# One key tile, scores against plain rotary products, and V by pairs in a latent-attention stage

## The chip, the cores and the metric

The kernel runs on one core of a Trainium2 chip. Its engines are TensorE (PE, the matmuls), VectorE (DVE), ScalarE (ACT), GpSimd (POOL) and SyncE (SP, which issues the DMAs). The metric is the device time of one execution in microseconds; three executions of the kernel before took 1416.03, 1418.67 and 1420.28 us. What differs by less than 0.3% (4.3 us) from the median is no measurable change.

## The reference, cut to what matters

```python
# SEQ 512, D_MODEL 1024, 8 heads, 128 plain + 64 rotary query/key dims, V 128, float32
def apply_rope(x, cos, sin):                       # x: ..., 64
    x1, x2 = x[..., :32], x[..., 32:]
    return concatenate([x1 * cos - x2 * sin, x2 * cos + x1 * sin], -1)

def mla(h, cos, sin, w_down, q_norm, w_uq, kv_norm, w_ukv, w_o):
    d = h @ w_down                                  # 1024 -> 384 + 128 + 64
    cq = rms_norm(d[..., :384], q_norm)
    ckv = rms_norm(d[..., 384:512], kv_norm)
    k_rope = apply_rope(d[..., 512:], cos, sin)     # one rotary key for all heads
    q = (cq @ w_uq).reshape(B, S, 8, 192)           # 128 plain, 64 rotary (apply_rope)
    kv = (ckv @ w_ukv).reshape(B, S, 8, 256)        # 128 key, 128 value
    ...                                             # causal softmax(q k / sqrt(192)) v
    return o.reshape(B, S, 1024) @ w_o

x = x + mla(rms_norm(x, norm_mix[1]), ...)          # between two SwiGLU stages
```

Around this stage stand, in program order, a pooling mixer, a SwiGLU feed-forward (1024 to 2816 and back), the attention stage, a second feed-forward, and a second block with two more attentions, gates and an output norm.

## The kernel before, in words

Activations are kept transposed: 128 features on the partitions, the 512 tokens along the row. Every float32 product is made of three matmuls (`triple`, L1590 to L1594): each operand is split into a rounded part `hi` (a copy by ACT into float32r) and the rest `lo` (a subtraction by DVE), and hi·hi, hi·lo and lo·hi are summed in PSUM. So a tile of 128 outputs over 8 input tiles (`chunk`) is 24 matmuls of 512 columns. Weights come in units of 128x2048 numbers: SP loads a unit when the one before the last is split, ACT makes `w_hi` (`split_hi`), DVE `w_lo` (`split_lo`); two buffers of each.

The attention stage, `mla` on each engine, has four parts.

1. Down-projection. Three weight units give six output tiles in banks 0 to 5: the key/value latent, one query latent tile, two tiles of the rotary key (the same 64 columns twice, plain and with its halves swapped, so that `key·cos + swapped·sin` is one rotated key on partitions 0 to 63 and again on 64 to 127), two more query latent tiles. DVE takes `1/rms` of the residual by a reciprocal (L1116) and multiplies each tile by it on its way out of PSUM (`down_q`, L1119, L1124).
2. First projections of a pair of heads, `FIRST_PROJ` (L308): plain key and query of head 0 (`kn0`, `qn0`), rotary queries of both heads (`u`) and the same with halves swapped (`us`), key of head 1 (`kn1`). A query or rotary tile takes 9 matmuls of 512 columns, a key tile 3, a value tile 12 of 128 columns (four token blocks of three). They alternate between banks 0 and 1; a projection waits until the one before the last is read.
3. 32 attention steps, four per head. Step s = (head h, ii) takes query block i = 3 - ii: `scores` (three matmuls of the plain part, three of the rotary part over 64 partitions, L1768, and a causal mask), with (i+1)·128 columns each, into one of three banks; the softmax is made by DVE (`row_max`), ACT (`softmax_exp`) and DVE (`normalise`); `turn(s-3)` transposes the probabilities of the step three before; ACT and DVE split them (`turned_hi`, `turned_lo`); `values` multiplies a whole head, in the first step of the head after next. At the end of a step come the projections for later heads that `after_step(h, ii)` lists (L310). Each engine goes through its own list in order; semaphores join them. A scores step waits for the exponentials of three steps before, and a turn for the `lo` of two turns before.
4. Output projection: 8 chunks of 24 matmuls, the first two begun between the last turns.

Names used below: `kn`, `qn`, `v` and a digit are the plain key, plain query and value of the even (0) or odd (1) head of a pair. `root`, `squares`, `sq_sum` are working tiles; `sq_sum` holds the partial sums of squares of the residual. `row_max` waits on `att_scored`, `turn` on `att_probs` and `att_lo`.

## Time and profile before

| | us |
|---|---|
| median of three runs | 1418.67 |
| the profiled execution's own time | 1417.11 |
| its span on the core | 1415.3 |
| PE busy in the span | 1352.3 (96%) |
| PE weight loads busy (beside the matmuls) | 1110.8 |
| DVE busy | 789.2 |
| ACT busy | 537.0 |
| POOL busy | 32.1 |

In the profile a PE row gives the time at which a matmul was issued and its modelled duration, which overlaps the next one's: what a matmul costs in a stream is the distance between two starts. L1592, L1593 and L1594 are the three lines of the helper `triple`, so its matmuls are told apart by the tiles behind the arrow. `[0.59 <-DVE pt_lo L1212]` behind a row is idle time of that engine just before it, and who ended it. `64*128` and `128*128` name the part of the array that a matmul uses. PEclk is the granted clock as a share of 2.4 GHz, so 0.50 is 1.2 GHz.

The attention stage runs from 404.22 us (first matmul of the down-projection) to about 600 us. Outside it the change touches only a few small constants that POOL writes at the start: POOL's last one is written at 0.90 us in the kernel before, and ACT's first read of one is at 10.34 us.

### The profile page before, as it was taken

Reading aid. Unit: us, or ns where it says so; the run is one execution under the profiler, and the core shown is the slowest. Engines: PE = TensorE matmul, PEld = TensorE weight load, DVE = VectorE, ACT = ScalarE, POOL = GpSimd, SP = SyncE. Lnnn points to the kernel's source line nnn. Section 1 sums busy time; section 2 is a strip of 40 time slices with the busy share of each in tenths; the row PEclk is TensorE's granted clock in tenths of the full one; section 3 lists DMA queues with packets and bytes.
Section 4 is the critical chain, followed back from the end, with each engine's and each line's share of the span. In section 5 each row is a group of like instructions: output and inputs, shape, how many; then the busy total and the mean of one; then the engine's idle time right before and its main releaser. Section 6 shows DMA issues by size and latency. Waiting matters only on the chain.

```text
span 1415.3 us, 16583 instructions
## 1 busy us (share of the span) xinstructions
PE 1352.3 (96%) x6315; PEld 1110.8 (78%) x6315; DVE 789.2 (56%) x1093; ACT 537.0 (38%) x754; POOL 32.1 (2%) x28
## 2 busy tenths in 40 slices
PE   6999999999999999899999999999999999977997
PEld 5788888888887777788888888888887787855876
DVE  5644445444456677465444454454775577876554
ACT  6522233233343444343222222334224345556334
POOL 6000000000000000000000000000000000020000
PEclk9999999999998999999999999999999999988999
DMA  6122322222342111032233222333542111102321
GB/s 207 60 94 96 107 89 89 93 82 89 98 119 55 31 44 47 32 117 90 96 98 103 89 82 82 104 99 104 152 144 82 60 31 45 61 0 89 117 78 60
DMA packets 130409, 120.75 MB, mean 85 GB/s; under 512 B 23020, under 2 KB 127416, under 8 KB 130104
## 3 DMA queue, kind: packets, MB, share of 16 engines
q1 hardware_dynamic: 130360, 120.08, 26.8%
q8 instruction: 33, 0.54, 0.2%
q14 instruction: 16, 0.13, 0.0%
HBM read 115.88 MB, written 4.19 MB: 85 GB/s over the span
## 4 chain that ended last, share of the span: by engine, by line
PE 86%; DVE 8%; ACT 3%; issue 2%; SPq 0%; DMA 0%; DVEq 0%; ACTq 0%
PE psum L1592 26%; PE psum L1593 26%; PE psum L1594 26%; DVE w_lo L1003 1%; PE psum L1936 1%; PE psum L1922 1%; PE psum L1908 1%; PE psum L1778 1%; ACT w_hi L577 1%; PE psum L1636 1%; PE psum L1769 0%; PE psum L2012 0%; PE psum L1628 0%; PE psum L1994 0%; DVE du L1269 0%
## 5 line engine op out<-in xcount | busy, mean ns | idle before, releaser
L1592 PE MATMUL psum<-xg_hi,w_hi 128*128 128x512 f32 x1080 | 429.2, 397 | 2.9 <-DVE xg_lo L1506 2.9
L1594 PE MATMUL psum<-xg_hi,w_lo 128*128 128x512 f32 x1080 | 420.7, 390 | 0.0
L1593 PE MATMUL psum<-xg_lo,w_hi 128*128 128x512 f32 x1080 | 420.6, 389 | 0.0
L1592 PEld LDWEIGHTS psum<-xg_hi,w_hi 128*128 128x128 f32 x1080 | 203.1, 188 | 46.0 <-DVE xg_lo L1506 3.4
L1594 PEld LDWEIGHTS psum<-xg_hi,w_lo 128*128 128x128 f32 x1080 | 202.8, 188 | 42.6
L1593 PEld LDWEIGHTS psum<-xg_lo,w_hi 128*128 128x128 f32 x1080 | 203.1, 188 | 40.8 <-issue 1.4
L1066 DVE TENSOR_TENSOR w_lo<-w_raw,w_hi 128x2048 fp32r<-128x2048 f32 x42 | 96.3, 2292 | 154.4 <-ACT w_hi L629 154.4
L1090 DVE TENSOR_TENSOR w_lo<-w_raw,w_hi 128x2048 fp32r<-128x2048 f32 x32 | 73.3, 2292 | 115.9 <-ACT w_hi L648 115.9
L1592 PE MATMUL psum<-act_hi,w_hi 128*128 128x512 f32 x352 | 137.2, 390 | 0.0
L1593 PE MATMUL psum<-act_lo,w_hi 128*128 128x512 f32 x352 | 137.0, 389 | 0.0
L1594 PE MATMUL psum<-act_hi,w_lo 128*128 128x512 f32 x352 | 136.9, 389 | 0.0
L629 ACT ACTIVATE w_hi<-w_raw 128x2048 fp32r<-128x2048 f32 x42 | 80.4, 1914 | 142.0 <-PE psum L1594 142.0
L1003 DVE TENSOR_TENSOR w_lo<-w_raw,w_hi 128x2048 fp32r<-128x2048 f32 (+2 forms) x60 | 95.1, 1586 | 29.5 <-ACT w_hi L577 29.5
L648 ACT ACTIVATE w_hi<-w_raw 128x2048 fp32r<-128x2048 f32 x32 | 61.2, 1913 | 117.6 <-PE psum L1594 117.6
L577 ACT ACTIVATE w_hi<-w_raw 128x2048 fp32r<-128x2048 f32 x40 | 76.4, 1909 | 25.8 <-PE psum L1594 25.7
L1592 PEld LDWEIGHTS psum<-act_hi,w_hi 128*128 128x128 f32 x352 | 66.1, 188 | 14.3 <-DVE w_lo L1090 0.6
L1594 PEld LDWEIGHTS psum<-act_hi,w_lo 128*128 128x128 f32 x352 | 66.1, 188 | 13.8
L1593 PEld LDWEIGHTS psum<-act_lo,w_hi 128*128 128x128 f32 x352 | 66.1, 188 | 13.5
L632 ACT ACTIVATE root<-squares 128x512 f32<-128x512 f32 x44 | 27.8, 632 | 100.4 <-DVE squares L1071 100.4
L634 ACT ACTIVATE act_hi<-squares 128x512 f32 (+1 forms) x44 | 27.8, 631 | 89.0 <-DVE squares L1076 89.0
L1073 DVE TENSOR_TENSOR squares<-psum,rstd 128x512 f32<-128x512 f32 x44 | 30.4, 691 | 50.4 <-PE psum L1594 50.4
L1079 DVE TENSOR_TENSOR act_lo<-squares,act_hi 128x512 f32 (+1 forms) x44 | 30.5, 693 | 39.9 <-ACT act_hi L634 39.9
(358 smaller groups left out, 1778.4 us busy)
## 6 DMA issues: line engine op xcount, KB each, us to landing
w_raw<-in_ffn_w_gate SPq DMA_DIRECT2D x22, 1024.0 KB, 5.0
w_raw<-in_ffn_w_up SPq DMA_DIRECT2D x22, 1024.0 KB, 4.9
w_raw<-in_w_in SPq DMA_DIRECT2D x16, 1024.0 KB, 5.5
w_raw<-in_ffn_w_down SPq DMA_DIRECT2D x16, 768.0 KB, 4.8
w_raw<-in_ffn_w_down SPq DMA_DIRECT2D x16, 640.0 KB, 4.3
w_raw<-in_mla_w_o SPq DMA_DIRECT2D x4, 1024.0 KB, 5.0
w_raw<-in_w_out SPq DMA_DIRECT2D x4, 1024.0 KB, 5.2
...
```

What stands on the lines that cost most here:

```text
L577: act.activation(w_hi[:, n % 2, :], raw(n), ACT.Copy).then_inc(hi_sem, 1)
L629: act.activation(w_hi[:, n % 2, :], raw(n), ACT.Copy).then_inc(hi_sem, 1)
L632: act.activation(gate_s, gate_z, ACT.Silu).then_inc(ga, 1)
L648: act.activation(w_hi[:, n % 2, :], raw(n), ACT.Copy).then_inc(hi_sem, 1)
L1003: lo = dve.tensor_tensor(w_lo[:, n % 2, c], raw(n)[:, c], w_hi[:, n % 2, c].bitcast(F32), ALU.subtract)
L1066: dve.tensor_tensor(w_lo[:, n % 2, :], raw(n), w_hi[:, n % 2, :].bitcast(F32), ALU.subtract).then_inc(lo_sem, 1)
L1073: dve.tensor_tensor(up_z, bank[2 + c][:, :], rstd[:, :], ALU.mult).then_inc(gd, 1)
L1079: dve.tensor_tensor(act_lo[:, f, :].rearrange("p a t -> p (a t)"), gate_z, act_hi[:, f, :].bitcast(F32).rearrange("p a t -> p (a t)"), ALU ...
L1090: dve.tensor_tensor(w_lo[:, n % 2, :], raw(n), w_hi[:, n % 2, :].bitcast(F32), ALU.subtract).then_inc(lo_sem, 1)
L1592: pe.matmul(o, wh, xh, start=start, stop=False, skip_group_check=True)
L1593: pe.matmul(o, wh, xl, start=False, stop=False, skip_group_check=True)
L1594: return pe.matmul(o, wl, xh, start=False, stop=stop, skip_group_check=True)
```

## The change

- **One key tile.** The down-projection makes five tiles, not six: one tile holds the 64 rotary key columns and, on the other 64 partitions, the same with swapped halves. From it come `K·cos` and `K·sin` as one 128-partition key that pairs with an unrotated product on the query side. Unit `KEY_UNIT` has 1024 columns to split instead of 2048.
- **Rotary scores from plain query times cos and sin.** The projection `us` is gone. From `u` (two heads of 64) DVE makes, for each head, `q·cos` on partitions 0 to 63 and `q·sin` on 64 to 127: four 64x512 products in place of two 128x512 products and a sum. ACT and DVE then split one 128-partition tile per head (`rotary(h)`), where one tile served two heads. The rotary scores run over all 128 partitions. A unit of head weights has 13·128 columns instead of 16·128.
- **Norms absorb the reciprocal root.** Query and key/value latents are no longer multiplied by `1/rms` of the residual; it would cancel in their own norms but for the epsilon, which comes in as a second accumulating matmul (`eps_share` times `sq_sum`) in both statistics. ACT and DVE read the latents in PSUM directly.
- **V by pairs.** A value projection makes two token blocks of both heads of a pair (`va`, `vb`): six matmuls of 256 columns, two such per pair, where there were two of twelve with 128 columns.
- **First steps reordered.** `FIRST_PROJ` is now `kn0, kn1, va, vb, u, qn0, qn1` in five banks, so that pair 0 has no projection left for heads 0 and 1; `after_step` and the two DVE/ACT places of `rotary` are new. On ACT a square of the key/value tile now stands ahead of the load of the square-root table.

On PE, in head 0, before: the end of `v0`'s twelve matmuls of 128 columns (`w_hi,ckv_hi`), then `scores(3)` (plain part from `xg_hi`, rotary part from `kr_hi`, mask), then `turn(0)`:

```order
L1592 MATMUL psum<-w_hi,ckv_hi 128x128
L1593 MATMUL psum<-w_lo,ckv_hi 128x128
L1594 MATMUL psum<-w_hi,ckv_lo 128x128
L1592 MATMUL psum<-xg_hi 128x128
L1593 MATMUL psum<-xg_lo,xg_hi 128x128
L1594 MATMUL psum<-xg_hi,xg_lo 128x128
L1592 MATMUL psum<-kr_hi,xg_hi 128x128
L1593 MATMUL psum<-kr_lo,xg_hi 128x128
L1594 MATMUL psum<-kr_hi,xg_lo 128x128
L1769 MATMUL psum<-causal,ident_r 128x128
L1778 MATMUL psum<-ident,probs 128x128 x4
```

On PE, the same place now: the end of `scores(2)`, then `scores(3)`, then `turn(0)`:

```order
L1650 MATMUL psum<-kr_lo,xg_hi 128x256
L1651 MATMUL psum<-kr_hi,xg_lo 128x256
L1831 MATMUL psum<-causal,ident_r 128x128
L1649 MATMUL psum<-xg_hi 128x128
L1650 MATMUL psum<-xg_lo,xg_hi 128x128
L1651 MATMUL psum<-xg_hi,xg_lo 128x128
L1649 MATMUL psum<-kr_hi,xg_hi 128x128
L1650 MATMUL psum<-kr_lo,xg_hi 128x128
L1651 MATMUL psum<-kr_hi,xg_lo 128x128
L1831 MATMUL psum<-causal,ident_r 128x128
L1840 MATMUL psum<-ident,probs 128x128 x4
```

`qn1` and `v0` no longer stand between the scores of steps 2 and 3 of head 0; they are made before `scores(0)`.

On DVE, in the second step of head 1, before: the rotary tile of the next pair (`u` times cos, `us` times sin, sum, `lo`), then `row_max`, `normalise` and `turned_lo` of the next step, then the `lo` of `qn0` and `v1`:

```order
L1167 TENSOR_TENSOR squares<-psum,cos_t 128x512
L1171 TENSOR_TENSOR squares<-psum,sin_t 128x512
L1173 TENSOR_TENSOR squares<-squares 128x512
L1180 TENSOR_TENSOR xg_lo<-squares,xg_hi 128x512
L1195 TENSOR_REDUCE row_top<-psum 128x1
L1197 TENSOR_TENSOR neg_max<-row_top,rq 128x1
L1202 RECIPROCAL row_inv<-row_sum 128x1
L1204 TENSOR_SCALAR probs<-probs,row_inv 128x384
L1212 TENSOR_TENSOR pt_lo<-psum,pt_hi 128x2x128
L1180 TENSOR_TENSOR xg_lo<-psum,xg_hi 128x512 x2
```

On DVE, the same place now:

```order
L1219 TENSOR_TENSOR squares<-psum,cos_t 64x512
L1220 TENSOR_TENSOR squares<-psum,sin_t 64x512
L1219 TENSOR_TENSOR squares<-psum,cos_t 64x512
L1220 TENSOR_TENSOR squares<-psum,sin_t 64x512
L1250 TENSOR_REDUCE row_top<-psum 128x1
L1252 TENSOR_TENSOR neg_max<-row_top,rq 128x1
L1257 RECIPROCAL row_inv<-row_sum 128x1
L1259 TENSOR_SCALAR probs<-probs,row_inv 128x384
L1267 TENSOR_TENSOR pt_lo<-psum,pt_hi 128x2x128
L1230 TENSOR_TENSOR xg_lo<-squares,xg_hi 128x512
L1225 TENSOR_TENSOR xg_lo<-psum,xg_hi 128x512
```

Two 128x512 products, a sum and a `lo` became four 64x512 products, and the `lo` of the rotary tile has moved behind `turned_lo` of the next step; `v1` is gone from here.

The diff, cut to what the text speaks of:

```diff
-        pieces = ((0, 2 * P, 2 * P), (256, 64, r0), (320, 64, r0), (384, 32, r0 + 32), (416, 32, r0), (448, 32, r0 + 32), (480, 32, r0),
-                  (512, 2 * P, 0))
+        pieces = ((0, 2 * P, 2 * P), (256, 64, r0), (320, 32, r0 + 32), (352, 32, r0), (512, 2 * P, 0))
...
 
         QUERY_TILES = (2, 0, 1)
-
-        FIRST_PROJ = ("kn0", "qn0", "u", "us", "kn1")
+        KEY_UNIT = FIRST["mla_down"] + 1
+
+        FIRST_PROJ = ("kn0", "kn1", "va", "vb", "u", "qn0", "qn1")
+        FIRST_BANKS = (5, 7, 0, 1, 2, 3, 0)
 
         def after_step(h, ii):
 
+            pr, last = h // 2, h + 1 == HEADS
             if h % 2 == 0:
-                return tuple((h // 2, what) for what in (("kn1",), (), ("qn1", "v0"), ())[ii] if h or what not in FIRST_PROJ)
-            return tuple((h // 2 + int(what != "v1"), what) for what in (("kn0",), ("u", "us"), ("qn0", "v1"), ())[ii] if what == "v1" or h + 1 < HEADS)
+                return () if h == 0 else (((pr, "kn1"),), (), ((pr, "qn1"),), ())[ii]
+            this = ((pr, "va"),), ((pr, "vb"),), (), ()
+            following = ((pr + 1, "kn0"),), ((pr + 1, "u"),), ((pr + 1, "qn0"),), ()
+            return (() if last else following[ii]) + (this[ii] if pr else ())
+
+        def rotary_head(h, ii):
+
+            if h % 2 == 0:
+                return h + 1 if h and ii == 1 else None
+            return h + 1 if ii == 2 and h + 1 < HEADS else None
 
         PROJ_ORDER = [(0, what) for what in FIRST_PROJ] + [x for h in range(HEADS) for ii in range(NB) for x in after_step(h, ii)]
 
+        def proj_bank(idx):
...
-                act.activation(w_hi[:, n % 2, :], raw(n), ACT.Copy).then_inc(hi_sem, 1)
+                if n == KEY_UNIT:
+                    hi = act.activation(tiles256(w_hi[:, n % 2, :], 8)[:, :, 0:P], tiles256(raw(n), 8)[:, :, 0:P], ACT.Copy)
+                else:
+                    c = slice(0, head_thirds(n)[-1])
+                    hi = act.activation(w_hi[:, n % 2, c], raw(n)[:, c], ACT.Copy)
+                hi.then_inc(hi_sem, 1)
...
+                act.wait_ge(sem("mla_down_done"), 1)
+                act.activation(squares[:, 0, :], bank[0][:, :], ACT.Square, scale=ROOT_KVL).then_inc(sem("kv_square"), 1)
...
+                    act.activation(cq_hi[:, t, :], bank[idx][:, :], ACT.Copy, scale=gain("mla_q_norm", t)).then_inc(sem("cq_act"), 1)
+                    act.activation(squares[:, n - 1, :] if n else sq_sum2[:, :], bank[idx][:, :], ACT.Square, scale=ROOT_QL).then_inc(sem("cq_act"), 1)
...
+                for what in FIRST_PROJ[:-1]:
+                    proj(0, what)
+                rotary(0)
...
+                dve.scalar_tensor_tensor(cos_s, cos_t[:, :], eps_col[:, 3:4], rstd[:, :], ALU.mult, ALU.mult).then_inc(step, 1)
+                dve.tensor_tensor(sin_s, sin_t[:, :], rstd[:, :], ALU.mult).then_inc(step, 1)
...
+                dve.tensor_tensor(down_q[:, 2, :], bank[2][:, :], cos_s, ALU.mult).then_inc(step, 1)
+                dve.tensor_tensor(root[0:64, :], bank[2][64:128, :], sin_s[64:128, :], ALU.mult).then_inc(step, 1)
+                dve.tensor_tensor(root[64:128, :], bank[2][0:64, :], sin_s[0:64, :], ALU.mult).then_inc(step, 1)
+                dve.wait_ge(step, 5)
+                dve.tensor_tensor(down_q[:, 2, :], down_q[:, 2, :], root[:, :], ALU.add).then_inc(*mark("kr_ready"))
...
+                        for e in range(2):
+                            r = slice(64 * e, 64 * e + 64)
+                            dve.tensor_tensor(squares[0:64, e, :], ps[r, :], cos_t[r, :], ALU.mult).then_inc(sem("rope_turned"), 1)
+                            sine = dve.tensor_tensor(squares[64:128, e, :], ps[r, :], sin_t[r, :], ALU.mult)
+                            sine.then_inc(*((done, 1) if e else (sem("rope_turned"), 1)))
                         return
...
+                def rotary(h):
+
+                    dve.wait_ge(sem("rope_hi"), h + 1)
+                    dve.tensor_tensor(xg_lo[:, QR + h % 2, :], squares[:, h % 2, :], xg_hi[:, QR + h % 2, :].bitcast(F32), ALU.subtract)\
+                       .then_inc(sem("rope_lo"), 1)
...
-                    pe.wait_ge(lo_sem, n + 1)
+                for idx, (j, c) in enumerate(((0, 1), (0, 0), (1, 0), (2, 0), (2, 1))):
...
+                    if idx == 1:
+                        pe.wait_ge(sem("kv_square"), 1)
+                        pe.matmul(bank[5][:, :], ones[:, :], squares[:, 0, :], start=True, stop=False)
+                        pe.matmul(bank[5][:, :], eps_share[:, :], sq_sum[:, :], start=False, stop=True).then_inc(*mark("kv_stat"))
...
+                            for j in range(2):
+                                tok = slice((2 * int(what == "vb") + j) * P, (2 * int(what == "vb") + j + 1) * P)
+                                o = ps[:, 2 * j * P:(2 * j + 2) * P].rearrange("p (e d) -> p e d", e=2)
+                                mm = triple(o, ckv_hi[:, tok], ckv_lo[:, tok], wh[:, 10:13:2, :], wl[:, 10:13:2, :], True, True)
...
-                            mm = pe.matmul(bank[6][:, 2 * i:2 * i + 2], sq_sum[:, i * P:(i + 1) * P], ones[:, 0:2], start=True, stop=True)
+                            tok = slice(i * P, (i + 1) * P)
+                            pe.matmul(bank[6][:, 2 * i:2 * i + 2], sq_sum2[:, tok], ones[:, 0:2], start=True, stop=False)
+                            mm = pe.matmul(bank[6][:, 2 * i:2 * i + 2], sq_sum[:, tok], eps_share[:, 0:2], start=False, stop=True)
...
-                    r = slice(64 * hs, 64 * hs + 64)
-                    qh, ql = rotary_q(h // 2)
-                    triple(o, qh[r, q], ql[r, q], kr_hi[r, k], kr_lo[r, k], False, False)
+                    triple(o, xg_hi[:, QR + hs, q], xg_lo[:, QR + hs, q], kr_hi[:, k], kr_lo[:, k], False, False)
```

## Rows read from the trace of the kernel before

**Rows 1.** The page's part 4: the chain that ended last, shares by engine.

```profile
PE 86%; DVE 8%; ACT 3%; issue 2%; SPq 0%; DMA 0%; DVEq 0%; ACTq 0%
```

**Rows 2.** Stretches: from:to, length, busy us (instructions) of PE, weight loads, DVE, ACT, POOL, granted clock, DMA.

```profile
438.66:450.08 11.42, 8.83 (x42) 6.85 (x41) 6.36 (x11) 4.88 (x8) 0.00 (x0) 0.99 0.24 51
450.08:480.89 30.81, 30.70 (x133) 23.64 (x134) 17.32 (x42) 11.53 (x25) 0.00 (x0) 0.78 0.15 35
480.89:511.75 30.86, 30.26 (x169) 24.30 (x168) 21.75 (x55) 14.83 (x34) 0.00 (x0) 1.00 0.11 35
511.75:542.63 30.88, 30.25 (x167) 24.32 (x166) 22.06 (x55) 14.85 (x34) 0.00 (x0) 1.00 0.10 35
```

**Rows 3.** Matmuls in order of time, 421 to 451 us: start, duration, line, tiles, shape.

```profile
421.45 1.02 PE L1717 MATMUL psum<-squares,ones 128*128 128x512 f32 x2
...
422.54 0.39 PE L1593 MATMUL psum<-xg_lo,w_hi 128*128 128x512 f32 x1
...
433.22 0.39 PE L1592 MATMUL psum<-xg_hi,w_hi 128*128 128x512 f32 x1
...
438.66 0.39 PE L1592 MATMUL psum<-ckv_hi,w_hi 128*128 128x512 f32 x1
...
450.08 0.76 PE L1592 MATMUL psum<-xg_hi 128*128 128x512 f32 x1 [2.31 <-DVE xg_lo L1180]
```

**Rows 4.** The same view, one 512-column scores step (head 1): plain, rotary, mask, turn.

```profile
466.12 0.40 PE L1594 MATMUL psum<-xg_hi,xg_lo 128*128 128x512 f32 x1
466.45 0.49 PE L1592 MATMUL psum<-kr_hi,xg_hi 64*128 64x512 f32 x1
466.78 0.39 PE L1593 MATMUL psum<-kr_lo,xg_hi 64*128 64x512 f32 x1
467.01 0.39 PE L1594 MATMUL psum<-kr_hi,xg_lo 64*128 64x512 f32 x1
467.34 0.33 PE L1769 MATMUL psum<-causal,ident_r 128*128 128x128 f32 x1
```

**Rows 5.** The same view: plain scores of 256 columns, and a value projection of 128 columns.

```profile
474.89 0.28 PE L1593 MATMUL psum<-xg_lo,xg_hi 128*128 128x256 f32 x1
475.01 0.28 PE L1594 MATMUL psum<-xg_hi,xg_lo 128*128 128x256 f32 x1
...
478.21 0.27 PE L1593 MATMUL psum<-w_lo,ckv_hi 128*128 128x128 f32 x1
478.32 0.28 PE L1594 MATMUL psum<-w_hi,ckv_lo 128*128 128x128 f32 x1
```

**Rows 6.** The same view: a turn that waits for DVE in the even head of a pair.

```profile
489.44 0.30 PE L1778 MATMUL psum<-ident,probs 128*128 128x128 f32 x1 [0.59 <-DVE pt_lo L1212]
```

**Rows 7.** Groups of 395 to 625 us: count, busy us, mean ns, idle before them.

```profile
L1180 DVE TENSOR_TENSOR xg_lo<-psum,xg_hi 128x512 fp32r<-128x512 f32 x24 | 16.6, 691 | 20.5 <-ACT xg_hi L687 20.2
L1212 DVE TENSOR_TENSOR pt_lo<-psum,pt_hi 128x512 fp32r<-128x512 f32 x8 | 5.5, 685 | 0.0
L1003 DVE TENSOR_TENSOR w_lo<-w_raw,w_hi 128x768 fp32r<-128x768 f32 x4 | 3.8, 946 | 0.0
L687 ACT ACTIVATE xg_hi<-psum 128x512 fp32r<-128x512 f32 x24 | 14.0, 596 | 9.0 <-PE psum L1594 9.0
```

**Rows 8.** Stretches, columns as in rows 2: around the falls of the granted clock.

```profile
448.00:450.00 2.00, 0.00 (x0) 0.00 (x0) 1.24 (x2) 1.11 (x2) 0.00 (x0) 0.96 0.00 0
450.00:452.00 2.00, 1.92 (x4) 1.20 (x5) 0.69 (x1) 0.00 (x0) 0.00 (x0) 0.50 0.00 0
...
462.00:464.00 2.00, 2.00 (x13) 1.90 (x12) 0.69 (x1) 0.60 (x1) 0.00 (x0) 0.63 0.00 0
...
562.00:566.00 4.00, 3.41 (x26) 3.02 (x26) 3.03 (x10) 1.63 (x5) 0.00 (x0) 0.99 0.32 115
...
566.00:568.00 2.00, 2.00 (x10) 1.76 (x10) 1.39 (x4) 1.20 (x4) 0.00 (x0) 0.50 0.00 0
...
586.00:590.00 4.00, 2.37 (x9) 1.61 (x9) 1.88 (x3) 2.51 (x2) 0.00 (x0) 1.00 0.00 0
```

More of the change, by code:

```diff
@@ L690, in mla @@
[L690 to L697 removed]
+                    h = 2 * pr + int(what[-1] == "1")
@@ L714, in mla @@
-                proj(0, "qn0")
+                act.activation(rq[:, 0, :], bank[6][:, 0:2 * NB], ACT.Sqrt, scale=128.0 + ROPE, bias=eps_col[:, 1:2]).then_inc(*mark("rq_root"))
+                proj(0, "qn1")
+                rotary(1)
                 act.preload_act_table(ACT.Exp)
-                for what in FIRST_PROJ[2:]:
-                    proj(0, what)
                 def softmax_exp(s):
@@ L1185, in mla @@
                 dve.wait_ge(*at("rq_ready"))
-                for what in FIRST_PROJ[1:]:
-                    proj(0, what)
+                proj(0, "qn1")
+                rotary(1)
                 def row_max(s):
@@ new lines, in proj @@
+                    if what[0] in "qu":
+                        if what == "u":
+                            pe.wait_ge(*at("kr_lo"))
+                        if idx == len(FIRST_PROJ) - 1:
+                            pe.wait_ge(sem("proj_ready"), 3)
+                        t0 = {"qn0": 0, "qn1": 3, "u": 6}[what]
+                        for i, k in enumerate(QUERY_TILES):
+                            pe.wait_ge(sem("cq_lo"), i + 1)
+                            mm = triple(ps, wh[:, t0 + k, :], wl[:, t0 + k, :], cq_hi[:, k, :], cq_lo[:, k, :], i == 0, i == 2)
@@ L1760, in scores @@
                         pe.wait_ge(sem("masks_ready"), 2)
-                    pe.wait_ge(sem("proj_ready"), proj_count(h // 2, *(("kn1", "qn1") if h % 2 else ("kn0", "qn0", "us"))))
+                    pe.wait_ge(sem("proj_ready"), proj_count(h // 2, f"kn{h % 2}", f"qn{h % 2}"))
+                    pe.wait_ge(sem("rope_lo"), h + 1)
                     if s >= 3:
```

201 lines of the change are left out of this document (97 added, 104 removed).

## The prediction, made before the changed kernel ran

> **What bounds the kernel now.** I read the chain of waits first: the chain that ended last is 86% PE [rows 1], so a matmul less is time less wherever PE has no gap. Next I cut the attention stage into stretches. In the middle of it (480.89 to 542.63) a pair of heads takes 30.9 us with PE busy 30.3 and DVE 21.8 to 22.1 [rows 2]: PE is the bound, with one regular wait of 0.59 us for `pt_lo` [rows 6], which says that DVE is close behind. Two stretches look different. Before the first scores PE is busy only 8.83 of 11.42 us, mostly for one wait of 2.31 us for the last `lo` of the first projections [rows 2, 3]. And heads 0 and 1 (450.08 to 480.89) ran at a mean granted clock of 0.78: it was 0.50, 1.2 GHz, from 450 us, right after 2 us without a matmul, and back at 2.4 GHz in the window 462 to 464 [rows 8]. From 450 to about 463.3 is 13.3 us at half speed with PE busy, some 6.7 us lost. It fell again at 566.
>
> **PE's own time, part by part.** 24 matmuls of 512 columns take 438.66 - 433.22 = 5.44 us, 0.227 each [rows 3].
> - The sixth down tile goes: -5.4.
> - `us` goes: 4 pairs x 9 x 0.227 = -8.2.
> - V: 8 heads x 12 = 96 matmuls of 128 columns at 478.32 - 478.21 = 0.11 become 4 x 12 = 48 of 256 columns. A 256-column matmul also starts 0.12 after the last (475.01 - 474.89) [rows 5]. So half the instructions cost half: -5.3.
> - Rotary scores over 128 partitions. A step inside one form takes 0.23; going from plain to rotary takes 466.45 - 466.12 = 0.33, the first rotary one 0.33, and rotary to mask 467.34 - 467.01 = 0.33 [rows 4]. With one form for all seven matmuls I take these 3 x 0.10 = 0.3 as gone: 32 steps, -9.6 at 512 columns, and I take -9 since the short steps show a little less. If they stay, because they belong to something else, the term is 0.
> - Added: a second float32 matmul in the kv statistic. The one there takes 422.54 - 421.45 = 1.09 with what it delays [rows 3]; the second costs between 0.45 and 1.09, I take 0.7. Four tiny pairs more in the query statistic, as much again: +1.5 together.
>
> Net -26.4 us of PE. Were PE the bound throughout and its first wait gone (-2.3), and the clock never fell before head 2 (-6.7), the gain would be 35. Most of the work is to find what DVE and the waits give back.
>
> A rule speaks against the V term. The rows show 0.11 at 128 columns as well, so here the trace disagrees with that formula for a stream in which every matmul loads weights, and I go by the trace.
>
> **Stage 1, to the first scores.** PE does 5.4 less of down-projection and +0.7 of statistic, then kn0, kn1, va, vb (12 x 0.227 or 0.11 x 2: 2.7), u, qn0, qn1 (27 x 0.227 = 6.1) and about 1.6 of statistic: 10.4 in place of 11.4 with the wait. Does anything come late? DVE splits 1024 columns fewer of the key unit and no longer multiplies the latents, so neither of its two long reciprocals stands between PE and the queries. On ACT the square now stands ahead of the square-root table load, so the reciprocal of the residual's norm starts some 1.1 us later; only the key's cos and sin need it, and the key is wanted 20 us on. The last `lo` before `scores(0)` is that of head 0's query and rotary tile. `qn1`, 2.0 us, lies behind them on PE and covers ACT 0.60 and DVE 0.69 twice [rows 7]. So scores start with no wait, at 450.08 - 5.4 + 0.7 - 1.0 = 444.3: -5.7. The POOL constants cost nothing: ready by about 1.4 us, read at 10.3.
>
> **Heads 0 and 1.** Before, 30.8 us at a mean clock of 0.78, 24.1 at full clock. Now head 0 has no projection at all: seven matmuls and a turn per step, 4.9 us for the head, and head 1 has kn0, u, qn0 of the next pair, 10.1 us. 15 us of PE against DVE: 17.3 before [rows 2], less three `lo` of 0.69 (qn1, v0, v1), plus two operations for the rotary tile: 16.6. The loop scores, row_max, exp, normalise, turn is now in the open: I get 19.7 us, taking step by step DVE's and ACT's order, with PE waiting in head 0 for the exponentials (ACT also splits the next head weights between exp(0) and exp(1)). Bounds: 16.6 (DVE alone) and 24. And the clock: in head 0 PE waits for exponentials several times in a row. Windows on both sides: it fell after 562 to 566 with PE 3.41 of 4 us busy, and did not after 586 to 590 with 2.37 of 4 [rows 8]. I give the fall 60% and its cost in a waiting stage as 3 to 6 us, and put in +3. So 30.8 becomes 22.7: -8.1.
>
> **Pairs 1 and 2.** PE's need falls from 30.3 by 2.04 (us) + 1.35 (V) + 8 x 0.28 (forms) = 5.7, with the 0.59 wait left 25.2. DVE needs 21.9 + 2 x 0.69 (four 64-partition products and two `lo` for two products, a sum and a `lo`) - 0.4 (weights 1664 for 2048 columns) = 22.9. The 64x512 product is not in the trace; it has 512 numbers per partition like the 128x512 one, so 0.69; between 0.28 (one of 128 columns) and 0.95 (one of 768 [rows 7]) it moves a pair by -1.6 to +1.0. V's copies with a stride: `pt_lo`, as split up, takes 0.685 against 0.691 [rows 7]: nothing. Both below 25.2, but the waits between them: in the odd head `qn0` takes the bank of `u`, which is free only after four products, 2.8 us, and PE has there only vb 0.7 and scores and turn of 0.9: 1.3 us of wait (before, it waited for one product). At the start of each head the scores need the `lo` of the last query: 0.2 + 0.60 + 0.69 with some DVE work ahead, against 1.2 us of PE work: about 0.5 twice. The turn in the even head waits some 0.4 longer. 25.2 + 1.3 + 1.0 + 0.5 = 28.0: -2.9 a pair, -5.8. Bounds: 25.2 (-11.4 for both) and 30 (-2).
>
> **Head 6, head 7 and the tail.** Head 6 -1.6 (it has `kn1` and `qn1`, loses half V and the forms, gains waits). Head 7: PE has little left, DVE's chain sets the steps; I get -1.5. The fall at 566 and the wait for the split weights of the output projection come at or after the end of the last head and stay.
>
> **Sum:** 5.7 + 8.1 + 5.8 + 3.1 = 22.7. From the profiled execution's 1417.1 this is 1394.4; that execution is 1.6 below the median of 1418.7, from which it would be 1396. I say 1395. Everything after 600 us is dense PE work that moves forward as a block.
>
> **Rivals.**
> - *PE stays the bound all through.* The waits I counted are hidden, the clock holds. For: before, DVE was busy 22 of 31 us and PE waited 0.6. Against: the margin is now 25.2 to 22.9. Pairs -11.4, no fall in head 0 (-3 more), its fall at 566 also milder: gain 28 to 34, 1383 to 1390. 15%.
> - *DVE and ACT bind from the first head on.* The chain takes 24 us in heads 0 and 1, pairs go to 30, the tail gives 0 to 1: gain 5.7 + 6.8 - 3 + 2 + 1 = 12.5, and 8 to 16 around it: 1401 to 1409. It includes the case that the 0.10 us gaps [rows 4] stay. 15%.
> - *The clock stays down: slower.* PE, which now waits somewhere in most steps, falls to 1.2 GHz in head 0 and does not come back until head 7. 24.6 us of PE work per pair become 49, +18 against before for each of pairs 1 and 2 and 9 for head 6: +45 - 5.7 - 8 = +31, 1448. It decides once PE is at half speed for more than about 45 us beyond before. For: the fall at 566 came from a stretch 85% busy. Against: at 463 it came back in the middle of the same pattern, and it then held 1.00 through both middle pairs, where PE also waited once a pair [rows 2, 6]. 4%. The Trainium skill's same page, "HAM oscillation", holds idle gaps between bursts of matmuls responsible; my largest one is 1.3 us, shorter than the 2.31 before the fall at 450, so by it there is no fall at all in heads 0 to 6 and the sum is 3 us better, 1392. The fall at 566, with no gap above 0.6, speaks against it as the whole rule.
> - *The change does nothing*: the first wait and the clock take back all that PE saves. It would need 22 us of new waits in stages that had 3. 3%.
>
> **Numbers.** Likeliest case, gain 16 to 28: 63%, 1390 to 1402 for itself. Range for 8 in 10: 1385 to 1403. Faster by over 0.3% (4.3 us, about what this measurement tells from nothing): 0.93; within: 0.03; slower: 0.04.
>
> **What would show it.** Right: 60 matmuls of 512 columns less, 48 of V, the rotary scores as `128*128` with 0.23 from start to start; first scores about 444 us without a wait; head 2 starting 13 to 17 us earlier than 480.89; pairs of 27 to 29 us with new PE waits on `squares` (the u products) and `xg_lo`; the end of attention 22 us earlier. Wrong: rotary steps still 0.33 apart, pairs near 25 or 30 us, a granted clock of 0.50 beyond 465 us, or PE gaps in the down-projection.

## The result and the profile after

The kernel after takes 1403.24 us (median of 4 runs, 1401.78 to 1406.12), beside 1418.43 us for the kernel before (4 runs, 1416.03 to 1420.28): ratio 0.9896, 95% interval 0.9879 to 0.9914. The forecast was 1395 us with a range of 1385 to 1403. The sign and the work removed are right; the gain is 8 us smaller than forecast, and the time lies just outside the range. The profiled execution took 1406.12 us, the slowest of the four, with a span of 1404.3.

The chain of waits that ended last has less PE in it and more of the others than in [rows 1]:

```profile
PE 83%; DVE 9%; ACT 4%; issue 3%; SPq 0%; DMA 0%; DVEq 0%; ACTq 0%
```

The stretches that answer to [rows 2], same columns: the projections of pair 0 up to the first scores; heads 0 and 1; pairs 1 and 2; head 6; and from head 7 to the output projection's wait for its split weights (in the kernel before the last two are 13.58 us and 34.76 us).

```profile
434.22:445.03 10.81, 10.81 (x62) 9.41 (x61) 8.17 (x13) 4.65 (x9) 0.00 (x0) 1.00 0.13 36
445.03:465.64 20.61, 16.00 (x92) 13.58 (x91) 16.60 (x42) 11.70 (x25) 0.00 (x0) 0.98 0.18 43
465.64:499.47 33.83, 28.84 (x145) 24.98 (x145) 22.83 (x58) 15.17 (x35) 0.00 (x0) 0.86 0.10 32
499.47:529.47 30.00, 24.77 (x145) 21.43 (x145) 22.74 (x58) 15.17 (x35) 0.00 (x0) 1.00 0.11 36
529.47:542.93 13.46, 10.59 (x62) 9.21 (x63) 9.30 (x26) 7.93 (x17) 0.00 (x0) 1.00 0.01 2
542.93:578.48 35.55, 28.59 (x141) 23.95 (x141) 16.61 (x41) 12.20 (x25) 0.00 (x0) 0.90 0.09 30
...
462.00:464.00 2.00, 0.90 (x9) 0.79 (x8) 1.65 (x6) 1.08 (x4) 0.00 (x0) 1.00 0.00 0
464.00:466.00 2.00, 0.88 (x5) 0.64 (x6) 1.67 (x5) 0.75 (x2) 0.00 (x0) 0.74 0.00 0
466.00:468.00 2.00, 2.00 (x6) 1.52 (x6) 0.60 (x3) 1.04 (x3) 0.00 (x0) 0.50 0.00 0
...
522.00:524.00 2.00, 1.19 (x11) 0.99 (x9) 1.91 (x3) 1.08 (x2) 0.00 (x0) 1.00 0.01 4
524.00:526.00 2.00, 1.03 (x5) 0.89 (x6) 1.94 (x4) 0.00 (x0) 0.00 (x0) 1.00 0.00 0
```

Pair 2 (499.47) shows the main point. PE has 24.77 us of work there, close to the 24.6 of the forecast, where it had 30.25. Yet the pair takes 30.00 us, where it took 30.88. PE lost 5.5 us of work and the pair lost 0.9. In pair 1 the granted clock falls on top of that. It reads 0.95 from 464.5 to 465 us and 0.50 from 465 on, so it fell about 0.5 us into an idle gap of 1.12 us; PE had been busy 0.90 of the 2 us from 462, and its gap before that one was 1.10 us. It falls once more at 482. At 522 to 526 PE is idle nearly as much and the clock stays.

PE's waits in pairs 1 and 2 (releaser, us in total, times, longest), with those before the first scores at both ends of the stretch; before there were two, of 0.59 us each, both like [rows 6]:

```profile
PE psum L1649 <- DVE xg_lo L1225: 4.3, 5, 1.1
PE psum L1840 <- DVE pt_lo L1267: 3.8, 4, 1.2
PE psum L1649 <- issue: 3.2, 2, 1.8
```

The "issue" ones are `qn0` waiting for the bank of `u`: the four 64-partition products that read it (half-products from here on) end on DVE right then. PE's own terms came out as forecast. Plain, rotary and mask matmuls now start 0.23 us apart where [rows 4] had 0.33, and V's 256-column matmuls 0.12, as [rows 5] had it:

```profile
436.80 0.28 PE L1650 MATMUL psum<-w_lo,ckv_hi 128*128 128x256 f32 x1
436.92 0.28 PE L1651 MATMUL psum<-w_hi,ckv_lo 128*128 128x256 f32 x1
...
445.49 0.39 PE L1651 MATMUL psum<-xg_hi,xg_lo 128*128 128x512 f32 x1
445.71 0.39 PE L1649 MATMUL psum<-kr_hi,xg_hi 128*128 128x512 f32 x1
445.94 0.39 PE L1650 MATMUL psum<-kr_lo,xg_hi 128*128 128x512 f32 x1
446.17 0.39 PE L1651 MATMUL psum<-kr_hi,xg_lo 128*128 128x512 f32 x1
446.39 0.22 PE L1831 MATMUL psum<-causal,ident_r 128*128 128x128 f32 x1
```

Why PE waits is seen in one step of head 4, all engines in order of time. `qn1` ends on PE at 510.02 and the next head's scores start at 512.60:

```profile
507.85 0.69 DVE L1230 TENSOR_TENSOR xg_lo<-squares,xg_hi 128x512 fp32r<-128x512 f32 x1 [0.56 <-ACT xg_hi L736]
508.46 0.82 DVE L1049 TENSOR_TENSOR w_lo<-w_raw,w_hi 128x640 fp32r<-128x640 f32 x1
509.19 0.68 DVE L1272 TENSOR_TENSOR o_lo<-psum,o_hi 128x512 fp32r<-128x512 f32 x1
509.62 0.40 PE L1651 MATMUL psum<-cq_hi,w_lo 128*128 128x512 f32 x1
509.79 0.41 DVE L1250 TENSOR_REDUCE row_top<-psum 128x1 f32<-128x256 f32 x1
...
510.44 0.57 ACT L764 ACTIVATE probs<-psum,neg_max,rq 128x256 f32<-128x256 f32 x1 [2.13 <-DVE neg_max L1252]
...
511.15 0.60 ACT L726 ACTIVATE xg_hi<-psum 128x512 fp32r<-128x512 f32 x1
511.41 0.63 PE L1840 MATMUL psum<-ident,probs 128*128 128x128 f32 x4 [0.67 <-DVE pt_lo L1267]
511.85 0.69 DVE L1225 TENSOR_TENSOR xg_lo<-psum,xg_hi 128x512 fp32r<-128x512 f32 x1 [0.59 <-ACT xg_hi L726]
...
512.60 0.49 PE L1649 MATMUL psum<-xg_hi 128*128 128x512 f32 x1 [0.57 <-DVE xg_lo L1225]
```

The row_max at 509.79 reads scores of 256 columns that PE had done at 506.25, but in DVE's list it stands behind a `lo` that waits for ACT, a weight split and `o_lo`. ACT idles 2.13 us for it; `qn1`'s `hi` stands behind that exponential in ACT's list, and DVE idles again for the `hi`. One chain of work runs through both engines in turns, and the pair takes longer (30.00 us) than either is busy (DVE 22.74, ACT 15.17).

### The profile page after: what moved, and what is told of

Read it like the earlier page. It is cut to its first block, busy times and chain, and to the rows that moved or that the text cites. A ratio compares the mean times of both kernels' runs of the same rounds, so it can differ in the third digit from the quotient of the medians.

```text
span 1404.3 us, 16380 instructions
## 1 busy us (share of the span) xinstructions
PE 1328.1 (95%) x6217; PEld 1099.4 (78%) x6217; DVE 788.8 (56%) x1098; ACT 536.7 (38%) x758; POOL 33.0 (2%) x32
## 4 chain that ended last, share of the span: by engine, by line
PE 83%; DVE 9%; ACT 4%; issue 3%; SPq 0%; DMA 0%; DVEq 0%; ACTq 0%
PE psum L1649 25%; PE psum L1650 25%; PE psum L1651 25%; DVE w_lo L1049 1%; PE psum L1998 1%; ACT w_hi L614 1%; PE psum L1984 1%; PE psum L1970 1%; DVE xg_lo L1225 1%; PE psum L2056 1%; PE psum L1693 1%; DVE du L1326 0%; PE psum L2092 0%; DVE row_top L1250 0%; PE psum L1917 0%
## 5 line engine op out<-in xcount | busy, mean ns | idle before, releaser
L667 ACT ACTIVATE w_hi<-w_raw 128x2048 fp32r<-128x2048 f32 x42 | 80.4, 1914 | 141.9 <-PE psum L1651 141.9
L1049 DVE TENSOR_TENSOR w_lo<-w_raw,w_hi 128x2048 fp32r<-128x2048 f32 (+4 forms) x59 | 90.8, 1540 | 29.0 <-ACT w_hi L614 28.9
L686 ACT ACTIVATE w_hi<-w_raw 128x2048 fp32r<-128x2048 f32 x32 | 61.2, 1913 | 117.6 <-PE psum L1651 117.6
L614 ACT ACTIVATE w_hi<-w_raw 128x2048 fp32r<-128x2048 f32 (+1 forms) x39 | 73.2, 1876 | 29.7 <-PE psum L1651 29.6
```

Of the source, the lines that this page charges most:

```text
L614: hi = act.activation(w_hi[:, n % 2, c], raw(n)[:, c], ACT.Copy)
L667: act.activation(w_hi[:, n % 2, :], raw(n), ACT.Copy).then_inc(hi_sem, 1)
L686: act.activation(w_hi[:, n % 2, :], raw(n), ACT.Copy).then_inc(hi_sem, 1)
L1049: lo = dve.tensor_tensor(w_lo[:, n % 2, c], raw(n)[:, c], w_hi[:, n % 2, c].bitcast(F32), ALU.subtract)
```

## The experiments

Times are compared as ratios to the kernel before, measured beside each on the same chip. "Pair 2" is heads 4 and 5. "Lost to the clock" is summed over 2 us stretches from 442 to 590 us of the one profiled execution, each with 2 x (1 - granted clock). It is rough, since time at half clock costs nothing where PE is idle. In runs 6, 7, 8 and 11 the clock also fell inside pair 2 (mean 0.95, 0.95, 0.90 and 0.95), so the length and PE's busy time there hold some of that.

| kernel | us | ratio, 95% | pair 2 | PE busy in it | lost to the clock |
|---|---|---|---|---|---|
| before | 1418 | 1 | 30.88 | 30.25 | 10.2 |
| after | 1403.2 | 0.9896 (0.9879 to 0.9914) | 30.00 | 24.77 | 8.5 |
| 1 before, one form | 1410.0 | 0.9946 (0.9930 to 0.9963) | 30.27 | 27.69 | 3.4 |
| 2 before, V wide | 1414.7 | 0.9976 (0.9965 to 0.9988) | 30.53 | 29.09 | 8.5 |
| 3 after, two products | 1397.6 | 0.9861 (0.9839 to 0.9884) | 28.24 | 24.79 | 5.1 |
| 4 after, gaps filled | 1400.4 | 0.9878 (0.9862 to 0.9895) | 30.01 | 29.67 | 0 |
| 5 after, products earlier | 1401.5 | 0.9870 (0.9834 to 0.9906) | 30.67 | 25.21 | 3.4 |
| 6 after, pt_lo earlier | 1414.0 | 0.9968 (0.9952 to 0.9984) | 32.41 | 25.84 | 11.9 |
| 7 both 5 and 6 | 1417.4 | 0.9982 (0.9966 to 0.9998) | 33.59 | 26.22 | 11.9 |
| 8 after, rotary 64 rows | 1417.4 | 0.9973 (0.9946 to 1.0000) | 34.32 | 30.48 | 17.1 |
| 9 after, lists reordered | 1389.9 | 0.9797 (0.9780 to 0.9813) | 27.50 | 24.24 | 1.7 |
| 10 as 9, filled | 1391.0 | 0.9807 (0.9788 to 0.9827) | 27.51 | 26.60 | 1.7 |
| 11 after, hi twice | 1411.6 | 0.9953 (0.9935 to 0.9972) | 31.93 | 26.21 | 8.5 |
| 12 as 9, hi twice | 1396.6 | 0.9847 (0.9815 to 0.9878) | 28.56 | 24.21 | 5.1 |

**1 and 2: two of PE's terms alone, in the kernel before.**

```diff
-                    triple(o, qh[r, q], ql[r, q], kr_hi[r, k], kr_lo[r, k], False, False)
+                    triple(o, qh[:, q], ql[:, q], kr_hi[:, k], kr_lo[:, k], False, False)
```

> The kernel before, with the rotary scores taken over all 128 partitions instead of the 64 of one head. The scores of the two heads of a pair are thereby summed; everything else stays. It tells what the three changes of row form per step are worth where TensorE is the bound. Theory (each change of form costs about 0.10 us on TensorE, 3 in each of 32 steps): 9 us less, 1409 us, with the three rotary matmuls and the mask 0.23 apart and pairs 1 and 2 going from 30.9 to about 28.4 us each. Rival (the 0.33 belongs to something else, or the DVE chain takes over at once): the steps stay 0.33 apart or the pairs stay at 30 or more, and the gain is 0 to 3 us.

```diff
-                            for j in range(NB):
+                            for j in range(2):
...
-                                mm = triple(ps[:, tok], ..., wh[:, t0, :], wl[:, t0, :], True, True)
+                                o = ps[:, 2 * j * P:(2 * j + 2) * P].rearrange("p (e d) -> p e d", e=2)
+                                mm = triple(o, ..., wh[:, t0 - 1:t0 + 1, :], wl[:, t0 - 1:t0 + 1, :], True, True)
```

> The kernel before, with each head's value projection done by 6 matmuls of 256 columns instead of 12 of 128 (half of the value rows are thereby wrong; the tile is written in full). Theory (a matmul of up to 256 columns starts 0.11 to 0.12 us after the last, whatever its columns): 48 matmuls less, 5.3 us less, 1413 us, pairs 1 and 2 at 29.6 us each. Rival (256 columns take twice as long as 128, as the isolated-matmul formula has it): no change in the time, matmuls 0.22 apart.

Run 1: the matmuls of a step start 0.23 us apart, so the 0.10 is the change of form. The total is 7.8 us less, near what the theory had, but for another reason. Pairs 1 and 2 with their waits in run 1:

```profile
474.92:505.34 30.42, 27.84 (x168) 24.16 (x166) 21.86 (x55) 14.86 (x34) 0.00 (x0) 1.00 0.11 36
505.34:535.61 30.27, 27.69 (x167) 24.18 (x167) 21.86 (x55) 14.83 (x34) 0.00 (x0) 1.00 0.11 35
```
```profile
PE psum L1778 <- DVE pt_lo L1212: 4.2, 6, 1.2
PE psum L1592 <- DVE xg_lo L1180: 1.0, 2, 0.5
```

PE has 2.4 to 2.6 us less work per pair and the pair is 0.4 to 0.6 shorter: the rest is back as waits for `pt_lo` and `xg_lo`. Most of the gain is the clock's. By the table 6.8 us less are lost to it, 5.1 of them in heads 0 and 1 (30.81 to 24.45 us), where it came back at about 455 us instead of 463, and the rest in head 7. So the total of run 1 doesn't tell what the forms are worth; the pairs do. Run 2 says the same: 256-column matmuls 0.12 apart, PE 1.2 us less per pair, the pair 0.35 less, the whole 3.0 where 5.3 was expected. The kernel before was already within 0.6 us of a second bound, near 30 us a pair.

**3: half of the new half-products.**

```diff
-                        for e in range(2):
-                            r = slice(64 * e, 64 * e + 64)
-                            ... cosine and sine product of rows r into squares[:, e, :]
+                        dve.tensor_tensor(squares[0:64, 0, :], ps[0:64, :], cos_t[0:64, :], ALU.mult)...
+                        dve.tensor_tensor(squares[64:128, 0, :], ps[0:64, :], sin_t[0:64, :], ALU.mult)...
```

> The kernel after, with two of the four half-products of the query's rotary tile left out (both heads of a pair use the tile of the first). Theory (DVE's products hold the bank that qn0 waits for, and their time comes straight off the wait): the 1.79 us wait before qn0 falls to about 0.4, pairs 1 and 2 fall by 1.4 us each, head 1 by up to 1.4, in all 3 to 5 us less than the kernel after, 1399 us. Rival (the wait only moves to the next thing, pt_lo or the scores of the next head): less than 1 us, 1403 us.

The theory holds: 5.0 us less by the ratios (the intervals overlap a little), pair 2 from 30.00 to 28.24 at a clock of 1.00 in both. Two half-products, which start 0.72 us apart, are 1.44 us of DVE; they came off the pair in full, and 0.3 more. By the table some 3.4 us of the total are the clock's.

**4: the gaps filled.**

```diff
+                def fill(s, n):
+                    if s >= 3:
+                        pe.wait_ge(sem("att_exp"), s - 2)
+                    for _ in range(n):
+                        pe.matmul(bank[2 + s % 3][:, :], ident_r[:, :], kr_hi[:, :], start=True, stop=True, ...)
```

> The kernel after, with matmuls added that do nothing of use (512 columns into a scores bank that is free, overwritten later), put where TensorE waited: 4 ahead of the first scores of heads 1 to 7, 5 and 3 ahead of the turns of the third and fourth step of even heads, of the fourth step of head 1 and of the last steps of head 7, and 7 ahead of each qn0. Theory (the granted clock fell at 464, 482, 544 and 557 us because of the gaps before): the granted clock stays at 1.00 from 464 to 500 us and at 543 to 547, which gives back 3.8 us in pair 1 and 1 to 2 in head 7, against up to 2 us by which the added matmuls overrun their gaps: 1399 to 1402 us. Rival (the falls do not come from the gaps): pair 1 keeps its two stretches at 0.50 and the time rises by the overrun, 1404 to 1407 us.

The stretches that fell in the kernel after, here:

```profile
464.00:466.00 2.00, 2.00 (x14) 1.73 (x14) 1.63 (x5) 0.80 (x2) 0.00 (x0) 1.00 0.00 0
466.00:468.00 2.00, 2.00 (x12) 1.67 (x11) 0.67 (x5) 1.04 (x3) 0.00 (x0) 1.00 0.00 0
...
482.00:484.00 2.00, 2.00 (x14) 1.87 (x13) 1.27 (x5) 1.25 (x3) 0.00 (x0) 1.00 0.61 161
```

The granted clock is 1.00 from 442 to 580 us, pair 1 goes from 33.83 to 29.53 us and pair 2 stays at 30.01 although PE has 4.9 us more to do in it. So the falls came from the gaps, and PE had nothing else to do in them. The end of the stretch comes 6.3 us earlier (572.17 for 578.48); of the whole time the ratios show 2.6 us, and their intervals overlap.

**5, 6 and 7: one wait at a time.**

```diff
-            following = ((pr + 1, "kn0"),), ((pr + 1, "u"),), ((pr + 1, "qn0"),), ()
+            following = ((pr + 1, "u"),), ((pr + 1, "kn0"),), ((pr + 1, "qn0"),), ()
...
-            return h + 1 if ii == 2 and h + 1 < HEADS else None
+            return h + 1 if ii == 1 and h + 1 < HEADS else None
```

> The kernel after, with the next pair's u and kn0 changing places in the odd head (u in its first step, kn0 in its second), and the rotary tile of the next head split a step earlier. qn0 then takes the bank of kn0 instead of that of u, and stands no more behind the four half-products. Theory (the 1.79 us before qn0 and most of the 1.01 before the next head's scores are waits of order, not of work): pair 2 from 30.0 to 27.5 us, with the two turns of the even head still waiting; heads 0+1 from 20.6 to 19.5; in all 5 to 8 us less than the kernel after, 1396 to 1398. Rival (DVE is the bound, so that the same time comes back at another wait, as the pt_lo of the odd head): pair 2 at 29.5 or more, 1401 or more.

```diff
-                    if 0 <= s - 4 < NB * HEADS:
+                    if s >= NB * HEADS and 0 <= s - 4 < NB * HEADS and s - 4 != NB * HEADS - 4:
                         turned_lo(s - 4)
...
                             proj(*t)
+                        if s >= 3:
+                            turned_lo(s - 3)
```

> The kernel after, with DVE's pt_lo of step s-3 done at the end of step s, behind the projections, instead of behind the first two groups of step s+1. Theory (the turns wait for pt_lo because of its place in DVE's list: DVE sits idle 1.77 us just before it): the waits of 1.17 and 0.67 us before the turns of even heads go, pair 2 from 30.0 to 28.2, the 2.18 before a turn behind head 7 gets shorter too; in all 4 to 6 us less than the kernel after, 1398. Rival (row_max then comes later, and with it the exponentials and the last lo before each head): the gain is under 1 us a pair, 1402.

> Both changes of order in one kernel: the next pair's u ahead of kn0 with the earlier split of the rotary tile, and pt_lo at the end of the step before. Theory (waits of order add up, TensorE's need of 24.8 us a pair is the next bound): pair 2 at 25.5 to 26.5 us, heads 0+1 at 19.5, head 6 at 12, in all 11 to 15 us less than the kernel after, 1388 to 1392, and the granted clock falls less often. Rival (DVE's 22.7 us with what its in-order list waits for is a bound near 28): pair 2 at 27.5 to 28.5 us, 1395 to 1397.

All three theories fell. In run 5 the 1.79 us before `qn0` became 1.00 before `kn0` (now behind the products) and 1.51 before `qn0`. Pair 2 is 0.67 us longer; the gain of 3.7 us by the ratios isn't sure (the intervals overlap), and the 5 us less that its execution loses to the clock are more than that. In run 6 the waits before the turns went, as meant, and 3.28 us stood before the next head's scores in their place:

```profile
513.62 0.56 ACT L764 ACTIVATE probs<-psum,neg_max,rq 128x256 f32<-128x256 f32 x1 [2.46 <-DVE neg_max L1252]
...
515.03 0.69 DVE L1225 TENSOR_TENSOR xg_lo<-psum,xg_hi 128x512 fp32r<-128x512 f32 x1 [0.92 <-ACT xg_hi L726]
...
515.78 0.79 PE L1651 MATMUL psum<-xg_hi 128*128 128x512 f32 x1 [3.28 <-DVE xg_lo L1225]
```

It is the chain shown above, only longer: `pt_lo`, now ahead of row_max on DVE, delays ACT's exponential, with it the `hi` behind it, and with that DVE. The even head of pair 2, nearly all of it at full clock, takes 13.92 us for 13.13; in the odd head (18.49 for 16.87) part of the growth is a fall of the clock, and run 7's pair 2 had one too. That gave the theory of runs 9, 11 and 12.

**8: the forms changed back, in the kernel after.**

```diff
-                    triple(o, xg_hi[:, QR + hs, q], xg_lo[:, QR + hs, q], kr_hi[:, k], kr_lo[:, k], False, False)
+                    triple(o, xg_hi[0:64, QR + hs, q], xg_lo[0:64, QR + hs, q], kr_hi[0:64, k], kr_lo[0:64, k], False, False)
```

> The kernel after, with its rotary scores on the first 64 rows of the tiles (the sine half of the rotary scores is left out), so that each step changes its row form three times again. It undoes the term of 9 us where the waits now are. Theory (5.2 us of a pair's time are waits that DVE and ACT set, so TensorE's extra 2.4 us vanish in them): pair 2 goes from 30.0 to 30.0 to 30.8 us, and the kernel is 0 to 3 us slower than the kernel after, 1403 to 1406. Rival (TensorE is still what the pairs pay for, as the prediction's sum took it): pair 2 at 32.4, 8 to 9 us slower, 1412.

Neither size came: 11 us slower by the ratios. Pair 2 is 34.32 us at a mean clock of 0.90; some 3.4 of that is the clock, and 30.9 is left, near the theory's upper end. The clock accounts for most of the total too: 17.1 us lost where the kernel after loses 8.5. Two of its ten executions took 1407 us, with a mean clock over the whole span (0.984 and 0.985) like the kernel after's (0.983 to 0.986); the eight of 1417 to 1419 had 0.975 to 0.977. So at a like clock the forms cost some 4 us here, between the theory's 0 to 3 and the rival's 8 to 9. Why the clock falls more often here, where PE has more work, the run doesn't tell.

**9: the chain cut, with the same instructions.**

```diff
+                    early = s % 2 == 1 and s - 4 < NB * HEADS - 4
+                    if early and s >= 4:
+                        turned_lo(s - 4)
+                    if here and ii == 1:
+                        for t in after_step(h, 0):
+                            proj(*t)
+                    if here:
                         row_max(s)
+                    if here and h % 2 == 0 and ii == 2:
+                        split_lo(FIRST["heads"] + 1 + h // 2, 0)
                     normalise(s - 1)
+                    if ii == 2 and h % 2 and h + 1 < HEADS:
+                        rotary(h + 1)
+                    if ii == 2 and s >= 10:
+                        head_out((s - 10) // NB)
...
                         softmax_exp(s)
+                        for t in after_step(h, ii):
+                            if t[1] in ("qn0", "qn1"):
+                                proj(*t)
```

(The first part is DVE's list, the last ACT's; the rotary `lo` of odd heads and `vb`'s `lo` also move to the third step, and ACT takes the rotary `hi` of even heads a step earlier.)

> The kernel after with the same instructions, in another order on DVE and ACT: DVE takes each row_max ahead of the lo of the projections of the step before (but those of the first step of a head), the rotary lo, vb's lo and o_lo move one step later, pt_lo of odd steps ahead of row_max; ACT takes the hi of qn0 and qn1 ahead of pt_hi, and the rotary hi of even heads a step earlier. Theory (a step's time is a chain that runs once through both engines: row_max, exponential, pt_hi, hi on ACT, then lo on DVE, and only then the next row_max, so that neither's busy time but their sum in turns sets the pair): with the chain cut, pair 2 goes from 30.0 to 27 or 28 us, heads 0+1 to 19, head 6 to 11.5 to 12.5, in all 8 to 12 us less than the kernel after, 1391 to 1395. Rival (DVE's own work is the bound, or each cut opens a wait elsewhere as in the two runs that moved pt_lo): pair 2 stays at 29.5 or more, 1401 to 1405.

1389.88 us, 13 less than the kernel after, with intervals far apart. Pairs 1 and 2, and PE's waits in them and at their end:

```profile
464.69:491.78 27.09, 24.24 (x148) 21.32 (x146) 22.75 (x58) 15.16 (x35) 0.00 (x0) 1.00 0.12 40
491.78:519.28 27.50, 24.24 (x145) 21.30 (x145) 22.74 (x58) 15.17 (x35) 0.00 (x0) 1.00 0.12 39
```
```profile
PE psum L1667 <- issue: 3.2, 2, 1.8
PE psum L1667 <- DVE xg_lo L1229: 1.9, 4, 0.5
PE psum L1858 <- DVE pt_lo L1271: 0.9, 2, 0.5
```

In pair 2 DVE is busy 22.74 us and ACT 15.17, to the hundredth as in the kernel after, and the clock is 1.00 in both; only the order differs, and the pair takes 2.5 us less. The step that was shown above, now:

```profile
499.04 0.42 DVE L1254 TENSOR_REDUCE row_top<-psum 128x1 f32<-128x256 f32 x1
...
500.49 0.57 ACT L764 ACTIVATE probs<-psum,neg_max,rq 128x256 f32<-128x256 f32 x1
500.83 0.68 DVE L1276 TENSOR_TENSOR o_lo<-psum,o_hi 128x512 fp32r<-128x512 f32 x1
...
501.03 0.61 ACT L726 ACTIVATE xg_hi<-psum 128x512 fp32r<-128x512 f32 x1
...
502.36 0.68 DVE L1229 TENSOR_TENSOR xg_lo<-psum,xg_hi 128x512 fp32r<-128x512 f32 x1
```

row_max comes ahead of `o_lo`, and neither engine idles in this step. Heads 0 and 1 take 19.05, head 6 11.46 us. The clock stays at 1.00 up to 540 us, although PE still waits 1.49 us before a turn in head 1 and 1.43 and 1.8 us before the `qn0` in pairs 1 and 2. So of the gain part is the clock's: of the 6.7 us in pair 1, 3.8 are what its falls had cost there. Several items moved at once, and no run tells what each is worth.

**10: the same with filled gaps.** The `fill` of run 4, 3, 6 and 6 matmuls in the places that the expectation names.

> The kernel with the reordered lists, with idle matmuls of 512 columns in its remaining long gaps: 3 ahead of the first scores of heads 1 to 7, 6 ahead of each qn0 and 6 ahead of a turn in the last step of heads 1 and 7. Theory (the granted clock follows the gaps): no stretch at 0.50 between 445 and 550 us; against the reordered kernel 0 to 3 us less, by as much as that one still loses at half clock minus some 1 us of overrun: 1390 to 1394. Rival (with shorter gaps the clock holds anyway): 0 to 2 us slower than the reordered kernel.

The rival came true: no gain (0.9807 for 0.9797, the same within the intervals). There was little left to give back (1.7 us lost to the clock in both), and the filling held up heads 0 and 1 (20.83 us for 19.05). The clock's one fall moved from 540 to 562 us, the wait for the output projection's weights, which wasn't filled.

**11 and 12: ACT's time as a probe.**

```diff
+                    if idx >= len(FIRST_PROJ) and what in ("kn1", "qn0", "qn1"):
+                        act.activation(proj_tiles(idx, xg_hi), proj_result(idx), ACT.Copy).then_inc(sem("hi_twice"), 1)
+                        act.wait_ge(sem("hi_twice"), ...)
                     act.activation(proj_tiles(idx, xg_hi), proj_result(idx), ACT.Copy).then_inc(sem("proj_hi"), 1)
```

> The kernel after, with ACT doing the hi of kn1, qn0 and qn1 of pairs 1 to 3 twice, one after the other (9 operations of 0.60 us more, 3 in each turn of two heads; the results are the same). ACT is busy 15.2 us of a pair's 30.0. Theory (a step is a chain through both engines in turn, so ACT's time counts although half of ACT is idle): each adds its 0.6 us to the pair, pair 2 from 30.0 to 31.3 to 31.8 us, and a fall of the clock may add to that; in all 3 to 6 us slower than the kernel after, 1406 to 1409. Rival (busy time of the busiest engine plus a few waits is what counts, and ACT has room): pair 2 stays at 30.0 to 30.4, 1403 to 1405.

> The kernel with the reordered lists, with the same 9 operations on ACT. Theory (the reordered lists have cut the chain at kn1, but qn0's and qn1's hi and lo are still what the next head's scores wait for, 0.48 us each): pair 2 goes from 27.5 to 28.0 to 28.6 us, less than in the kernel after; 1391 to 1393. Rival (the chain is not cut, the reordering gained by something else): the same 1.3 to 1.8 us a pair as there.

Both theories hold in the pairs: pair 2 grows by 1.93 us in the kernel after, for 1.8 us of work on an engine that is idle half of the time, and by 1.06 with the lists reordered. In run 11 the clock fell in the even head of pair 2, so part of the 1.93 may be that. The heads in which it didn't fall settle it: head 5 grows by 0.61 us (16.87 to 17.48) for one operation of 0.60, head 6 by 1.25 (13.46 to 14.71) for two. In run 12 they grow by 0.40 and 0.71. In the whole time both are worse than expected, 8.1 and 7.1 us slower by the ratios. In run 12 the falls of the clock came back: 5.1 us lost for 1.7, and pair 1 took 31.35 us at 0.89. In run 11 no more is lost to it than in the kernel after (8.5 us); its trace shows 4.1 us between the first scores and the end of head 6 and 2.2 before the first scores, where the edit changes nothing. The rest isn't explained.

## Why the prediction was right or wrong

**Right.** PE's terms: 60 matmuls of 512 columns and 48 of V less, the forms (runs 1 and 2, and the rows of the profile after). Only V's term was a little too large: 96 x 0.11 less 48 x 0.12 is 4.8 us, not 5.3, and run 2 has 1.2 a pair for 1.35. The first stage: scores start at 445.03 with no wait, 5.05 us earlier, forecast 5.7. Head 2 starts 15.25 us earlier, within the 13 to 17 forecast.

**Right by luck in part: heads 0 and 1.** They take 20.61 us, for which 19.7 was worked out and 3 added for a fall of the clock that the forecast gave 60%. The clock held until the last 0.7 us of head 1, so 10.2 us were gained where 8.1 was forecast.

**Wrong: the term of pairs 1 and 2.** This is the step that failed: "25.2 + 1.3 + 1.0 + 0.5 = 28.0: -2.9 a pair." PE's work was right: busy 24.8, and 25.2 less the old wait of 0.6 is 24.6. The waits were 5.2, not 3.4: `qn0` 1.79 for 1.3, the scores of the two heads 0.57 + 1.01 for 1.0, the turns 1.17 + 0.67 for the old 0.6 and 0.5 more. So pair 2 took 30.00 us where 28.0 was forecast. The sum was made wait by wait, each from what its releaser had to do, with the engines compared by busy time (25.2 against 22.9). But in a pair DVE waits for ACT and ACT for DVE in turns. Runs 1 and 2 show a bound near 30 us already in the kernel before, hidden 0.6 us behind PE. Run 3 shows that time taken off DVE comes off the pair in full, run 11 that time put on ACT is added in full, and run 9 that the order of the lists makes the bound: 27.5 us with the same work. It was a rival in the forecast, "DVE and ACT bind from the first head on", with "pairs go to 30", a gain of 8 to 16 us and 15%. Pair 2 (30.00 us) and the total came true as it had them, but the total by luck: its sum of 12.5 us has heads 0 and 1 at 24 us, which took 20.61, and no fall of the clock in pair 1, which took 33.83.

**Wrong: where the clock falls.** 3 us were put into heads 0 and 1, where it held, and none after; it fell at 465 and 482 and cost pair 1 3.8 us against pair 2, and again in head 7. The forecast had named "a granted clock of 0.50 beyond 465 us" as a sign that it was wrong. Run 4 shows that the gaps did it. The forecast had argued from its largest gap being short; the first fall came about 0.5 us into a gap of 1.12 us, behind one of 1.10, the second after gaps of 0.82 and 0.56. The Trainium skill, in "TensorE: Matmul & The Clock Gate", section "HAM oscillation", blames idle gaps between bursts: run 4 agrees with that much, but the reading that "by it there is no fall at all in heads 0 to 6" is refuted by 0.50 from 465 on. The length of a gap alone doesn't decide it either: the gaps of pair 2 were 1.17, 0.67, 0.57 and 1.79 us, and the clock stayed at 1.00. Why it fell in pair 1 and not there stays unexplained.

**The accounts.** Gained up to the output projection's wait: 12.5 us (578.48 for 590.97) where 22.7 was forecast. Of the 10.2 missing, pair 1 is 5.9 (3.0 more instead of 2.9 less), pair 2 2.0, head 6 1.5, head 7 and tail 2.3, the first stage 0.6; heads 0 and 1 gave 2.1 back. Behind that point this one execution loses 1.5 us against that of before. The 421.5 us that follow do move as a block, as forecast, but not the rest: behind 1230 us PE is not dense (5.99 of 10 us at 1250) and the clock falls in both kernels, at other moments. The medians, 15.2 apart, show more gain than these two executions.
